# Reading and writing the columns of the feed-forward and output projection matmuls four by four from two halves

## What is computed

```python
# first block
h = h + jnp.einsum('bsd,de->bse', merged, w_out[l])              # proj_out 1
u = jnp.einsum('bsd,df->bsf', rmsnorm(h, norm_ffn_g[l]), w_up[l])  # up 1
u = causal_depthwise_conv(u, conv_w[l], conv_b[l])
gate, val = jnp.split(u, 2, axis=-1)
h = h + jnp.einsum('bsf,fd->bsd', jax.nn.silu(gate) * val, w_down[l])  # down 1
# second block, on 16 meta tokens and the 512 tokens
h = h + 0.5 * swiglu(rms_norm(h, norm_ffn1[l]), w_ffn1_in[l], w_ffn1_out[l])  # up 2, down 2
h = h + token_mixer(...)                                         # ends with proj_out 2
h = h + 0.5 * swiglu(rms_norm(h, norm_ffn2[l]), w_ffn2_in[l], w_ffn2_out[l])  # up 3, down 3
```

## Time and profile before

| | us |
|---|---|
| median of 3 runs | 2252.72 (2252.37 to 2254.26) |
| span of the profiled execution | 2252.2 |
| PE busy | 2204.9 (98%) |
| DVE busy | 1239.3 (55%) |
| ACT busy | 904.3 (40%) |
| line 1171 in the chain that ended last | 53% of the span |

### The profile page before, as it was taken

How to read it: one execution, slowest core, us unless ns; L and a number is a source line. 1 busy time by engine, 2 the same in 40 slices (tenths; PEclk the granted TensorE clock), 3 DMA queues, 4 the chain that set the end, 5 groups by cost and what they waited for, 6 DMA issues and landing times.

```text
span 2252.2 us, 35995 instructions
## 1 busy us (share of the span) xinstructions
PE 2204.9 (98%) x12576; PEld 1815.6 (81%) x12576; DVE 1239.3 (55%) x2661; ACT 904.3 (40%) x1815; POOL 222.4 (10%) x201
## 2 busy tenths in 40 slices
PE   8999999999999999999999899999999999999998
PEld 6567766778888889999999788887777787888887
DVE  6778776567727745543443555544555555443442
ACT  5565444444414443222232344444444433322332
POOL 0100044310000031000001000121100130000001
PEclk9999999999999999999999999999999999999999
DMA  4112212234533342333333223343433233332332
GB/s 123 35 41 57 52 43 57 82 111 146 155 107 94 113 127 76 93 122 90 93 95 104 62 82 91 84 105 94 99 100 96 77 104 88 94 108 86 94 102 76
DMA packets 400394, 205.93 MB, mean 91 GB/s; under 512 B 66909, under 2 KB 393929, under 8 KB 400285
## 3 DMA queue, kind: packets, MB, share of 16 engines
q1 hardware_dynamic: 399365, 204.09, 31.7%
q10 hardware_dynamic: 919, 0.43, 0.1%
HBM read 202.21 MB, written 14.80 MB: 96 GB/s over the span
## 4 chain that ended last, share of the span: by engine, by line
PE 84%; DVE 3%; ACT 2%; issue 1%; POOL 0%; DVEq 0%; ACTq 0%; POOLq 0%
PE acc L1171 53%; PE acc L1477 17%; PE acc L1221 5%; PE sco L1512 2%; PE acc L1576 1%; PE acc L1572 1%; PE sco L1265 1%; PE sco L1552 1%; PE acc L1312 1%; DVE w_lo L2276 1%; PE acc L1552 1%; PE sco L1532 0%; PE acc L1299 0%; DVE bias L2264 0%; PE sco L1289 0%
## 5 line engine op out<-in xcount | busy, mean ns | idle before, releaser
L1713 ACT ACTIVATE w_hi<-raw 128x512 fp32r<-128x512 f32 (+4 forms) x656 | 372.0, 614 | 694.5 <-PE acc L1171 660.1
L2276 DVE TENSOR_TENSOR w_lo<-raw,w_hi 128x512 fp32r<-128x512 f32 (+4 forms) x656 | 424.4, 687 | 141.0 <-ACT w_hi L1713 136.4
L1171 PE MATMUL acc<-xn_hi,w_hi 128*128 128x512 f32 (+1 forms) x1408 | 421.1, 340 | 2.1 <-DVE qbuf L2843 2.1
L1171 PE MATMUL acc<-xn_lo,w_hi 128*128 128x512 f32 (+1 forms) x1408 | 422.1, 340 | 0.0
L1171 PE MATMUL acc<-xn_hi,w_lo 128*128 128x512 f32 (+1 forms) x1408 | 420.3, 339 | 0.0
L1171 PEld LDWEIGHTS acc<-xn_hi,w_hi 128*128 128x128 f32 x1408 | 241.9, 188 | 35.7 <-DVE qbuf L2843 3.0
L1171 PEld LDWEIGHTS acc<-xn_lo,w_hi 128*128 128x128 f32 x1408 | 241.2, 188 | 31.2 <-issue 0.5
L1171 PEld LDWEIGHTS acc<-xn_hi,w_lo 128*128 128x128 f32 x1408 | 241.5, 188 | 30.0
L1171 PE MATMUL acc<-hid_lo,w_hi 128*128 128x512 f32 (+1 forms) x832 | 261.5, 349 | 0.0
L1171 PE MATMUL acc<-hid_hi,w_lo 128*128 128x512 f32 (+1 forms) x832 | 260.5, 347 | 0.0
L1171 PE MATMUL acc<-hid_hi,w_hi 128*128 128x512 f32 (+1 forms) x832 | 259.8, 347 | 0.8 <-DVE hid_lo L2785 0.8
(11 more groups left out here) (399 smaller groups left out, 3044.2 us busy)
## 6 DMA issues: line engine op xcount, KB each, us to landing
raw<-in_w_ffn_in SPq DMA_DIRECT2D x176, 256.0 KB, 3.0
raw<-in_w_in SPq DMA_DIRECT2D x118, 256.0 KB, 3.1
raw<-in_w_up SPq DMA_DIRECT2D x88, 256.0 KB, 3.0
raw<-in_w_ffn_out SPq DMA_DIRECT2D x32, 384.0 KB, 3.4
raw<-in_w_gate SPq DMA_DIRECT2D x48, 256.0 KB, 3.1
raw<-in_w_ffn_out SPq DMA_DIRECT2D x32, 320.0 KB, 3.7
raw<-in_w_out SPq DMA_DIRECT2D x32, 256.0 KB, 2.9
bias<-grids_dram SPq DMA_DIRECT2D x64, 128.0 KB, 3.0
```

The source lines that it names most:

```text
L1171: mm = pe.matmul(acc[0:m, 2 * slot + b, 0:size], w[slot][:, t, 0:m], x[:, place(t), c:c + size], start=(t == 0 and w is w_hi and x is xh), ...
L1713: act.activation(w_hi[slot][:, a:b, :], raw[slot][:, a:b, :], ACT.Copy).then_inc(S[f"hi_ready{slot}"], parts)
L2276: dve.tensor_tensor(w_lo[slot][:, a:b, :], raw[slot][:, a:b, :], w_hi[slot][:, a:b, :].bitcast(F32), ALU.subtract).then_inc(S[f"split{slot ...
```

## The change

`item` reads its columns and writes its bank in another order. A helper splits the columns of an access pattern into two halves (`a`), each half into groups of four (`g`, `c`), and walks over the groups with the two halves in turn: four columns of the first half, four of the second, the next four of the first. It is applied to the PSUM operand and to the moving operand, so that each column is written where it was written before. The weights, the number of matmuls and all waits are as they were.

```diff
+            def by_fours(ap):
+
+                return ap.rearrange("p (a g c) -> p g a c", a=2, c=4)
+
             def item(slot, k, tiles, m, xh, xl, blk, x_ready=None, place=lambda t: t):
...
                         for b, (c, size) in enumerate(segs(blk)):
-                            mm = pe.matmul(acc[0:m, 2 * slot + b, 0:size], w[slot][:, t, 0:m], x[:, place(t), c:c + size],
+                            mm = pe.matmul(by_fours(acc[0:m, 2 * slot + b, 0:size]), w[slot][:, t, 0:m],
+                                           by_fours(x[:, place(t), c:c + size]),
                                            start=(t == 0 and w is w_hi and x is xh),
                                            stop=(t == tiles - 1 and w is w_lo))
```

## The result

The kernel after takes 2353.75 us (median; 2353.43 to 2354.37), the kernel before beside it 2253.49 us: a ratio of 1.0443, 95% interval 1.0431 to 1.0456. It is 100 us slower where 40 us less was forecast. The time lies inside the range, on the side of the rivals.

A forecast was written before the change was run, and what follows sets the result against it. PE was taken to bound the kernel, by line 1171's matmuls times their pace. One term, 21.3 + 19.0 = 40 us for 512 and 264 columns, gave 2252.7 - 40 = 2212 us, range 2168 to 2460.

The forecast's parts named there:

- What bounds the kernel: PE, 98% busy with 84% of the chain; line 1171 alone 53% of the span, its matmuls times their pace 1210 us.
- ACT's wait for the line: ACT's weight split waits 660.1 us for line 1171; this wait should change by about the whole difference in time.
- the loss depends on where PE reads: On line 1171, part of the loss follows the tile's address: 388 against 396 ns for the same tensors and shape.
- reading two halves in turn makes the walk through each half go at half the speed, and meets it about half as often: Reason for the gain on line 1171: a walk through memory meets something unknown at regular places; 40 us less, chance 0.50.
- A gain of 6 ns a matmul: Line 1171: every matmul at the best tiles' pace, 388 instead of 394 ns and 279 instead of 285; 40 us less.
- The scale of the possible gain: Line 1171 takes 104 us above one column a clock; at best 88.5 us of it could be gained.
- Nothing moves: Rival for line 1171: the order of columns is of no account; time stays 2252.7 us; chance 0.13.
- Slower, by leaving a stretch of adjoining columns more often: Rival for line 1171: one clock lost at each step between stretches of 16 columns; 205 us more, 2457 us; chance 0.27.
- Much slower, the bank: Rival for line 1171: the bank can't take a broken order at a column a clock; +1008 us, 3261 us; chance 0.10.
- The chances: Odds for the whole kernel's time by the 0.2% that a measurement can tell: faster 0.50, same 0.13, slower 0.37.

The follow-up runs named there:

- The swept order: Kernel before, changed line read and written in forward sweeps of runs of four, 16 columns apart for 512, 12 for 264: 2226.92 us against 2252.29, ratio 0.9884.

## Why the prediction was wrong, point by point

- What bounds the kernel was right: time is the number of matmuls on the line times their pace. The pace was slower by 20.2 and 9.1 ns, which makes 101 us, against 99.5 us of span. No other engine became late; ACT's wait for the line grew by nearly the whole difference, as the prediction said it would.
- That the loss depends on where PE reads the earlier trace rows was right. The step that failed is the one after it: "reading two halves in turn makes the walk through each half go at half the speed, and meets it about half as often". In its place the runs show a price that hangs on which addresses follow one another, and two halves 256 columns apart are one of the dearer pairs: 252.1 ns against 231.9 for one run and 242.2 at a distance of 240 columns. A gain of 6 ns a matmul was taken from the tile that fares best; it was a loss of 20.2 with 512 columns and of 9.1 with 264.
- The scale of the possible gain was sound: 104 us lie above the column clock, and an order can take some back. The swept order took 25 us of it on the line, less than the 40 us forecast, and it is another order than the one forecast to give them.
- "Nothing moves" fell with the pace. The Trainium skill, page "Advanced Engine Details and Errata", section Memory Cachelines, gives SBUF lines of 16 bytes, full performance where following accesses hit the same line, and a need of at least two hits on a line. The trace agrees in part: every other run of four, each a full line, kept 231.9 to 233.0 ns. But runs of two, which hit a line twice, rose to 328.3 and 435.0 ns, and full lines from two places took 240 to 253 ns, at some steps 272 to 307. So neither two hits nor a full line is enough.
- "Slower, by leaving a stretch of adjoining columns more often" had the right sign, and its range reached the result at about half of its full price (100 of 205 us). Its mechanism is wrong: steps to other stretches cost 1 ns at most in every other run, and at a step of 16 columns, where every run lies in another stretch, the pace fell to 228.3 ns.
- "Much slower, the bank" was wrong. The Trainium skill, page "PSUM — Partial Sum Buffer", section Specifications (TRN2), says that an order in the bank that isn't contiguous slows matmuls significantly; here all ten orders of the bank stayed within 0.3 ns of the same stage of before, and the measurement decides.
- The chances were badly set. One row of a size in the trace, 388 against 396 ns, said that addresses matter and nothing of the direction; half the chance on a gain leant on an argument, not on a row.

What stays open is why. It was shown that reading alone does it, that neither the start of the read, nor breaks, nor open stretches explain it, that narrower weight loads take only some 3 of 20 ns away with 512 columns (and 3 of 9 with 264), and that steps of whole 256 bytes are dear. Which conflict makes 20, 24 and 52 columns dear, and 24 only in passes of six and more, isn't settled; no rule tried here covers all the orders. It wasn't shown either why one and the same swept stream takes 222.8 ns at one time and 228.3 at another.

## What to carry to other kernels

Where PE sets the end and its pace stands a few per cent above a column a clock, the order in which the moving operand is read is a lever of its own, worth here from -1.7% to +22%: try orders on the chip, one a stage of one kernel, before any is built in. Keep runs of at least four fp32 columns, and don't alternate between two places, above all not where the step there or the step back is a multiple of 256 bytes, as it was for the halves of 512 and of 264 columns. No order of the bank tried here cost anything with this operand type, so the bank can be written in whatever order the read takes.

## What was not expected of the hardware

- One run from end to end isn't the fastest read: 231.9 ns for 512 columns, against 222.8 to 228.3 when every fourth run of four is taken in four passes; 264 columns 122 against 119.6 to 120.1.
- Runs of two, each in another 16 bytes than the run before, take 435.0 / 256 = 1.70 ns a run at a step of 16 columns, 4.1 clocks at 2.4 GHz, and 328.3 / 256 = 1.28 ns, 3.1 clocks, from two halves in turn. So a change of line has no fixed price; whether a line has a shortest time wasn't shown.
- A step of 24 columns in passes of sixteen makes the same matmul a third slower (306.7 ns), in passes of four not at all (233.3).
- One tile read again and again takes 226.7 to 233.5 ns by tile, but with the high part of every tile moved to such a start, 512 columns took 232.2 ns.
- The same stream of matmuls, with the same addresses in the same order, ran at 228.3 ns a matmul in one kernel and at 222.8 in another, steadily in both.
